# A hybrid decoder step on one core: conv taps from PSUM on two engines, key sums spread anew, query rows by DMA, prompt q/k turned inside units 17 to 24

## The reference

```
h = rmsnorm(x) @ w_in           # 1024 -> conv channels 1536, z 512, b/a 8, q, k, v 512 each, two gates 1024 each
q,k,v of branch A = silu(causal_conv4(conv channels))       # y[t] = sum_i x[t-3+i] * w[i], per channel
branch A = gated DeltaNet(q, k, v, g, beta) -> gated rmsnorm -> w_proj_a
branch B: q, k = partial rope; prompt: causal attention (blocks of 256)
          sample: scores of q with the MEAN of each block of 256 cached keys choose 3 blocks per head,
                  softmax over the chosen blocks and the own row, times cached values; -> w_proj_b
h = x + (sigmoid(ga) * A + sigmoid(gb) * B) @ w_out;  y = h + relu(rmsnorm(h) @ w_up)^2 @ w_down;  final rmsnorm
```

## Time and profile before

| | |
|---|---|
| median of 3 runs | 1262.8 us (1260.28 to 1270.4) |
| span of the profiled execution | 1264.6 us, its first to its last instruction; the change is weighed against this |
| busy share | TensorE 89%, its weight loads 82%, VectorE 53%, ScalarE 36%, GpSimd 20% |
| mean granted clock of TensorE | 0.915 of 2.4 GHz (0.5 is 1.2 GHz) |
| DMA | 151.06 MB, mean 119 GB/s |

### The profile page before, as it was taken

How to read it: one execution, slowest core, us unless ns; L and a number is a source line. 1 busy time by engine, 2 the same in 40 slices (tenths; PEclk the granted TensorE clock), 3 DMA queues, 4 the chain that set the end, 5 groups by cost and what they waited for, 6 DMA issues and landing times.

```text
span 1264.6 us, 21204 instructions
## 1 busy us (share of the span) xinstructions
PE 1125.7 (89%) x8030; PEld 1037.6 (82%) x8030; DVE 674.7 (53%) x906; ACT 460.8 (36%) x686; POOL 257.4 (20%) x112
## 2 busy tenths in 40 slices
PE   4999778787999777997997899999999999999995
PEld 3979778775666666976885879999999999999995
DVE  3526899987643457558554433655533443433433
ACT  3333243333244255455443413324432422522422
POOL 0018455567500006344433000000000000000000
PEclk9989888886579789997997889999999999999998
DMA  7427556566510004464554613432232323232321
GB/s 253 152 65 203 184 184 200 159 201 181 150 43 17 20 25 124 135 183 133 147 153 121 204 34 117 131 120 85 88 97 86 99 85 99 83 99 83 100 66 68
DMA packets 179079, 151.06 MB, mean 119 GB/s; under 512 B 8881, under 2 KB 141555, under 8 KB 178870
## 3 DMA queue, kind: packets, MB, share of 16 engines
q1 hardware_dynamic: 133416, 122.12, 31.9%
q10 hardware_dynamic: 45590, 27.93, 7.7%
HBM read 141.19 MB, written 8.91 MB: 119 GB/s over the span
## 4 chain that ended last, share of the span: by engine, by line
PE 63%; DVE 6%; ACT 4%; issue 2%; POOL 1%; DMA 1%; ACTq 0%; DVEq 0%; POOLq 0%
PE ps L407 44%; PE ps L1729 6%; PE ps L1716 4%; PE ps L1606 2%; PE ps L1616 2%; PE ps L1630 2%; POOL v_low L548 1%; DVE v_low L1212 1%; ACT v_high L783 1%; PE ps L1836 1%; ACT w_high L391 1%; DMA out<-yy 1%; PE ps L1697 1%; PE ps L1823 1%; PE ps L1843 0%
## 5 line engine op out<-in xcount | busy, mean ns | idle before, releaser
L391 ACT ACTIVATE w_high<-w_raw 128x1024 fp32r<-128x1024 f32 x125 | 132.3, 1059 | 461.9 <-PE ps L407 422.8
L407 PE MATMUL ps<-xh,w_high 128*128 128x256 f32 x1232 | 268.9, 301 | 25.9 <-DVE w_low L396 25.9
L407 PE MATMUL ps<-xl,w_high 128*128 128x256 f32 x1232 | 260.3, 294 | 0.0
L407 PE MATMUL ps<-xh,w_low 128*128 128x256 f32 x1232 | 259.4, 293 | 0.0
L396 DVE TENSOR_TENSOR w_low<-w_raw,w_high 128x1024 fp32r<-128x1024 f32 x125 | 162.1, 1297 | 173.9 <-ACT w_high L391 173.6
L407 PEld LDWEIGHTS ps<-xh,w_high 128*128 128x128 f32 x1232 | 204.0, 202 | 37.2 <-DVE w_low L396 21.6
L407 PEld LDWEIGHTS ps<-xl,w_high 128*128 128x128 f32 x1232 | 204.1, 201 | 0.0
L407 PEld LDWEIGHTS ps<-xh,w_low 128*128 128x128 f32 x1232 | 203.0, 199 | 0.0
L531 POOL TENSOR_TENSOR ring<-ring,qb 128x1024 f32<-128x1024 f32 x64 | 162.4, 2555 | 177.3 <-ACT qb L660 90.1
L407 PE MATMUL ps<-mh,w_high 128*128 128x256 f32 (+1 forms) x640 | 129.3, 283 | 2.4 <-issue 2.4
L548 POOL TENSOR_TENSOR v_low<-ring,v_high 128x1024 fp32r<-128x1024 f32 x32 | 79.7, 2490 | 249.3 <-ACT v_high L783 249.3
(11 more groups left out here) (349 smaller groups left out, 1475.5 us busy)
## 6 DMA issues: line engine op xcount, KB each, us to landing
ring<-in_cache_k SPq DMA_DIRECT2D x128, 256.0 KB, 3.2
ring<-in_cache_v SPq DMA_DIRECT2D x128, 256.0 KB, 2.8
w_raw<-in_w_in ACTq DMA_DIRECT2D x82, 256.0 KB, 4.3
w_raw<-in_w_up SPq DMA_DIRECT2D x64, 256.0 KB, 3.1
w_raw<-in_w_down SPq DMA_DIRECT2D x64, 256.0 KB, 3.0
w_raw<-in_w_out SPq DMA_DIRECT2D x16, 256.0 KB, 3.1
ht_dram<-ht ACTq DMA_DIRECT2D x1, 2080.0 KB, 8.1
ht<-ht_dram SPq DMA_DIRECT2D x8, 260.0 KB, 3.6
```

The lines of the kernel that those rows point to most:

```text
L391: act.activation(w_high[:, u % 2], w_raw[:, s], ACT.Copy).then_inc(S_hi, 1)
L407: last = pe.matmul(out[:, a:b], w[:, u % 2, k, :], x[:, i, a:b], start=(first + i == 0 and w is w_high and x is rhs_h), stop=(first + i == ...
```

## The change

- **Conv taps.** `pre` and its zeroing go. ScalarE writes the last tap itself: it copies the sums into `cvr` scaled by that tap's weight (`tap_out`). VectorE adds the other three with the sums read straight from PSUM, each over the columns that have a predecessor. ScalarE waits for the free `cvr` (`tm_turned`), and TensorE's unit u+2 waits for `conv_out` of unit u, because its place in PSUM is read until then. `cvr` moves into the place of `ht`, so its first uses wait for `ht_kept`.
- **Key sums.** None before unit 8; two in units 8 to 12, one or two by turns (18 in 12 units) in 13 to 24, two in 25 to 28: 36. The other 28 are taken in the attention, one a step.
- **Query rows.** The eight matmuls and copies go. SP writes the 8 rotated rows (16 KB) to DRAM and reads them back into all 128 partitions (2 MB), ahead of the fifth key group. GpSimd waits for `qb_landed`.
- **Prompt q/k.** The eight times four transposes and their copies move to units 17 to 24, one each behind `turn_conv`, in banks 6 and 7; ScalarE's wait for the four stores of keys and values moves to unit 17. Gate 0 follows unit 28 directly.

```diff
--- before.py
+++ after.py
 GROUPS = NS * NPAGE // 2
-RED_STEP0 = 6
-RED_T1 = 2 * (N1 - RED_STEP0)
+U_C, U_Z, U_TURN = 13, 25, 17
+
+
+def keys_in_unit(u):
+
+    return 0 if u < 8 else 2 if u < U_C or u >= U_Z else 1 + u % 2
...
+    qb_dram = nc.dram_tensor("qb_dram", [NS, WB], F32, kind="Internal").ap()
...
-        pre = at("pre", [P, 2, 3 + SEQ], F32, r1 + 71872)
-        cvr = at("cvr", [P, 2, SEQ], F32, r1 + 76000)
+        cvr = at("cvr", [P, 2, SEQ], F32, ht_at + 2 * NT * 4)
...
+            def keep_queries():
+
+                sp.wait_ge(*done("rope_q"))
+                sp.dma_start(qb_dram, mts[:, 0:WB]).then_inc(qb_kept, 16)
+                sp.wait_ge(qb_kept, 16)
+                sp.dma_start(qb[:].rearrange("p b c -> p (b c)"),
+                             bc(qb_dram.rearrange("(o b) c -> o (b c)", o=1), [P, NS * WB])).then_inc(qb_landed, 16)
...
                 for r in range(8):
@@ -458,6 +470,8 @@
                         taken, count = low_done(r + 4)
                         sp.wait_ge(taken, b * 4 + (count - 4))
                     elif r >= 4 or not first:
+                        if first and r == 4:
+                            keep_queries()
                         sp.wait_ge(S["k_red"], base + (r - 3))
                     for i in range(2):
...
-            g.wait_ge(S["qb_out"], NS)
+            g.wait_ge(qb_landed, 16)
...
                 elif kind == "c":
                     if j == 0:
-                        act.wait_ge(*done("scr_out"))
-                        act.wait_ge(*done("pre_zero"))
+                        act.wait_ge(ht_kept, 16)
+                        act.wait_ge(*done("own_out"))
                     if j >= 2:
-                        act.wait_ge(S["conv_out"], j - 1)
-                    link(A(pre[:, j % 2, 3:3 + SEQ], unit_ps(u % 2)[:, 0:SEQ], ACT.Copy))
+                        act.wait_ge(S["tm_turned"], j - 1)
+                    A(cvr[:, j % 2], unit_ps(u % 2)[:, 0:SEQ], ACT.Copy,
+                      scale=fw[:, R_CW + 36 + j:R_CW + 37 + j]).then_inc(S["tap_out"], 1)
                     A(tail[:, j], unit_ps(u % 2)[:, SEQ - 3:NT], ACT.Copy).then_inc(unit_out, 1)
                     if j >= 1:
                         silu(j - 1)
@@ -654,10 +669,6 @@
                         conv_turned_out(10)
                     if j == 1:
                         conv_turned_out(11)
-                if u in (5, 6):
-                    for b in range(4 * (u - 5), 4 * (u - 5) + 4):
-                        act.wait_ge(S["qb_sums"], b + 1)
-                        A(qb[:, b], bank(4 + b % 4), ACT.Copy).then_inc(S["qb_out"], 1)
...
+                if U_TURN <= u < U_TURN + 8:
+                    if u == U_TURN:
+                        act.wait_ge(stored_kv, 64)
+                        act.wait_ge(*done("own_out"))
+                        act.wait_ge(qb_kept, 16)
+                        act.wait_ge(*done("ba_out"))
+                    n = u - U_TURN
+                    act.wait_ge(S["qk_turned"], n + 1)
+                    A((qt if n < 4 else kt)[:, n % 4], bank(6 + n % 2), ACT.Copy, scale=ATT_SCALE if n < 4 else 1.0)\
+                        .then_inc(S["qk_out"], 1)
...
-            act.wait_ge(stored_kv, 64)
-            act.wait_ge(*done("own_out"))
-            for n in range(8):
-                act.wait_ge(S["qk_turned"], n + 1)
-                if n == 0:
-                    act.wait_ge(S["conv_out"], 12)
-                    act.wait_ge(*done("ba_out"))
-                A((qt if n < 4 else kt)[:, n % 4], bank(n % 4), ACT.Copy, scale=ATT_SCALE if n < 4 else 1.0)\
-                    .then_inc(S["qk_out"], 1)
-                if n == 3:
-                    gate(0)
+            gate(0)
...
-            v.wait_ge(*done("scr_out"))
-            v.memset(pre[:, :, 0:3], 0.0).then_inc(*did("pre_zero"))
...
             def conv(j):
-                u = 13 + j
+                u = U_C + j
+                v.wait_ge(S["tap_out"], j + 1)
                 v.wait_ge(unit_out, u + 1)
-                if j >= 2:
-                    v.wait_ge(S["tm_turned"], j - 1)
-                c, x = cvr[:, j % 2], pre[:, j % 2]
+                c, x = cvr[:, j % 2], unit_ps(u % 2)
                 w = [fw[:, R_CW + 12 * i + j:R_CW + 12 * i + j + 1] for i in range(CW)]
-                link(TS(c, x[:, 0:SEQ], w[0], None, ALU.mult))
-                link(STT(c, x[:, 1:1 + SEQ], w[1], c, ALU.mult, ALU.add))
-                link(STT(c, x[:, 2:2 + SEQ], w[2], c, ALU.mult, ALU.add))
-                STT(c, x[:, 3:3 + SEQ], w[3], c, ALU.mult, ALU.add).then_inc(S["conv_out"], 1)
+                for back in (1, 2, 3):
+                    ins = STT(c[:, back:SEQ], x[:, 0:SEQ - back], w[3 - back], c[:, back:SEQ], ALU.mult, ALU.add)
+                    if back < 3:
+                        link(ins)
+                    else:
+                        ins.then_inc(S["conv_out"], 1)
...
+                    v.wait_ge(ht_kept, 16)
...
-                if u >= RED_STEP0:
-                    reduce_keys(n_red, 2)
-                    n_red += 2
+                reduce_keys(n_red, keys_in_unit(u))
+                n_red += keys_in_unit(u)
...
-            v.wait_ge(*done("own_out"))
             split_low(v, U_GATE + 2)
...
+            def turn_moba_heads(n):
+                if n == 0:
+                    pe.wait_ge(S["mts_out"], 12)
+                    pe.wait_ge(*done("ba_out"))
+                    pe.wait_ge(S["rope_k"], 2)
+                if n >= 2:
+                    pe.wait_ge(S["qk_out"], n - 1)
+                turn4(6 + n % 2, [mtqk[:, t, n * P:(n + 1) * P] for t in range(4)]).then_inc(S["qk_turned"], 1)
+
             for u, (kind, j, _) in enumerate(UNITS1):
                 pe.wait_ge(S_lo, u + 1)
                 if u >= 2:
                     pe.wait_ge(unit_out, u - 1)
+                if U_C <= u - 2 < U_Z:
+                    pe.wait_ge(S["conv_out"], u - 1 - U_C)
...
-                    pe.wait_ge(*done("rope_q"))
-                if u in (5, 6):
-                    for b in range(4 * (u - 5), 4 * (u - 5) + 4):
-                        if b == 0:
-                            pe.wait_ge(S["mt_out"], 4)
-                            pe.wait_ge(S["mts_out"], 4)
-                        if b == 3:
-                            pe.wait_ge(*done("ba_out"))
-                        if b >= 4:
-                            pe.wait_ge(S["qb_out"], b - 3)
-
-                        mm(bank(4 + b % 4), bc(cf[0:NS, K_ID + b:K_ID + b + 1], [NS, P]), mts[:, 0:WB],
-                           start=True, stop=True).then_inc(S["qb_sums"], 1)
                 if u >= 1 and UNITS1[u - 1][0] in "qkv":
                     turn_moba((u - 1) - (1 if u - 1 > 4 else 0))
                 if kind == "c" and j >= 2:
                     turn_conv(j - 2)
                 if kind == "z" and j < 2:
                     turn_conv(10 + j)
+                if U_TURN <= u < U_TURN + 8:
+                    turn_moba_heads(u - U_TURN)
...
+            pe.wait_ge(S["qk_out"], 8)
+            gate(0)
             pe.wait_ge(unit_out, N1)
-            pe.wait_ge(S["rope_k"], 2)
-            for n in range(8):
-                if n >= 4:
-                    pe.wait_ge(S["qk_out"], n - 3)
-                turn4(n % 4, [mtqk[:, t, n * P:(n + 1) * P] for t in range(4)]).then_inc(S["qk_turned"], 1)
-                if n == 3:
-                    gate(0)
 
             def scores(n):
                 q_t, h = divmod(n, HB)
                 r, N = slice(64 * (h % 2), 64 * (h % 2) + 64), (q_t + 1) * P
-                if n < 3:
-                    pe.wait_ge(S["qk_out"], 8)
-                else:
+                if n == 2:
+                    pe.wait_ge(S["tm_out"], 12)
+                if n >= 3:
                     pe.wait_ge(S["att_exp"], n - 2)
                 mm(score_bank(n, N), qt[r, h // 2, q_t * P:(q_t + 1) * P], kt[r, h // 2, 0:N], start=True, stop=True)\
                     .then_inc(S["att_sums"], 1)
```

12 lines of the change are left out of this document (5 added, 7 removed).

## The result

The changed kernel takes 1219.0 us in the median of four runs (1214.3 to 1221.8), the kernel before 1261.5 on the same chip. The ratio is 0.968, 95% interval 0.964 to 0.972: 3.2% faster. The prediction was 1215 us, in a range of 1201 to 1236, and faster by over 1%. The profiled execution has a span of 1214.4 us, 50.2 less than the 1264.6 of before; the medians differ by 42.6. In every execution that has both on record the time is 1.8 us above the span.

What follows compares the result with a forecast made beforehand. VectorE was taken to bound the conv and z units, TensorE most other stretches. -14.0 - 30.4 - 5.65 + 2 = -48.1 from 1264.6 gave 1216.5, less 1.8 for the median: 1215 us, range 1201 to 1236.

Steps and rivals of the forecast that it cites:

- (a): Units 6 and 7: query rows by DMA instead of matmuls, 12.6 us instead of 26.59, -14.0.
- (e): Attention: key sums go from 18 to 28 and fit VectorE's waits; products may hold dg or w_low, +2 us.
- (c): Conv units, unit 13 to 28: PSUM taps at 0.75 us, TensorE the longer; 100.5 against 130.89 us, -30.4.
- (b): Units 8 to 12: time from unit 7 to 13 left as it was; up to 4 us could go by luck.
- rival C: Conv units: taps from PSUM wait for GpSimd all the same, +60 us, 1275; chance 0.05.
- the slips: Units 13 to 28: 3 us added to 97.5 for new waits, among them held w_low and a late conv(2).
- (d): Hand-over from unit 28's end to the attention's first exp: 10.05 us instead of 15.7, -5.65.
- rival B: Attention steps 9 to 17: clock stays at 2.4 GHz, some 8 us shorter, 1205 with some luck; chance 0.07.
- Rivals A: Conv units stay fed too slowly and settle at 7.5 us, adding 12 us: 1227; chance 0.14.
- D: Conv stage never bound by VectorE, TensorE's gaps from key loads; only (a) and (d) count: 1243; chance 0.05.

Runs made afterwards that it cites:

- e9: Kernel before with only the query rows by DMA (eight matmuls and copies gone): 1248.3 us, ratio 0.990.
- e6: Changed kernel with the small gate instructions early, key rotation spread over units 10 to 12, some key sums moved, store of k in unit 13: 1209.8 us, ratio 0.962.
- e4: Kernel before with GpSimd's products over 16 of their 1024 columns: 1213.5 us, ratio 0.963.
- e10: Changed kernel with GpSimd's products over 16 of their 1024 columns: 1204.8 us, ratio 0.955.
- e2: Changed kernel with ScalarE copying to SBUF again and four VectorE taps reading there: 1234.3 us, ratio 0.978.
- the square: Four kernels: before and changed, each with full and with small GpSimd products; unit 13 to 28 took 130.9, 103.5, 92.8 (before, small) and 96.9 us (changed, small).
- e5: Changed kernel with VectorE's three small gate instructions moved from unit 13 to behind the copy of ba after unit 4: 1213.8 us, ratio 0.965.
- e11: Changed kernel with the prompt's q and k turned behind unit 28 as before, not in units 17 to 24: 1217.0 us, ratio 0.963.
- e3: Changed kernel with two key sums in every unit from 8 on, 22 left for the attention: 1218.5 us, ratio 0.964.
- e7: Changed kernel with the attention's diagonal (dg) made by ScalarE instead of VectorE: 1222.0 us, ratio 0.973.
- e8: Changed kernel with the edits of e6 and e7 together: 1213.5 us, ratio 0.965.

## Why the prediction was right

The largest part came by the mechanism named: taps that read PSUM are not held, and TensorE sets the pace of the conv units. For (a) and (e) the number was better than the reason. 48.1 us were forecast; 50.2 came in the spans and 42.6 in the medians, whose interval allows 36 to 46. So 48.1 is a little too much, and the closeness of the spans is in part luck: before was profiled in one of its longer executions, after in one of its shorter, and the errors of the parts cancel, 3.0 us of gain too much in (c) against 1.5 too little in (b), 2.5 in (e) and 1.1 in the rest. The 1.8 us that I took off for the median are by the later runs what an execution takes beyond its span, not what a median lies below it; for the forecast this changes nothing, since it is the median of before less 48.1 either way.

(a) 14.0 forecast, 14.0 measured (26.59 to 12.63), and e9 gives it by itself. But the matmuls are not short, as I called them: they took 8.4 of the 14.0 us, and the low clock cost the two products 4.8. The row that I read shows five of their sixteen instructions. The forecast didn't need the split, since it took the whole difference to two undisturbed units. The clock did fall without a hole: from 78 to 83 us of before TensorE is busy all the time and the granted clock is 0.53, right behind the first group of 8-row matmuls. The broadcast took 6.9 us, nearer the 8.1 of the store of its size than the 19.6 of four times wf; the 16 KB before it, taken at 3.2, were over in at most 2.3 (issue at 70.82, next issue at 73.16), close to the 2 us of the Trainium skill, DMA: Bandwidth & Descriptors, section Latency and other measured facts.

(b) Left as it was, with up to 4 us of luck: 1.5 less. That the hole behind unit 12 would stay was right (6.9 us); e6 shows that it needs the rotation, e4 and e10 that it needs the products beside it.

(c) 100.5 forecast, 103.5 measured. The taps at 0.75 are right to the hundredth, and rival C is dead: e2 and the square show that the place of one operand decides. The Trainium skill, VectorE: DVE Perf Modes, section Rules for kernel authors, has to copy to SBUF first as one of two ways if many operations follow; here that form costs 17.9 us more (e2). The Trainium skill, SBUF — State Buffer, section Who interferes with whom, gives the reason, and the traces agree: two SBUF inputs, up to 2.85 us; one in PSUM, 0.751 at most. The step that was mis-sized is the slips. I allowed 3 us over the ideal 97.5: 0.34 a unit for w_low and 1 us late for conv(2) in unit 14. Measured are 6.9 over four undisturbed units up to T(17), and 0.9 under the estimate behind it. w_low was held (1.75 us in the mean of the stage's 15) and cost nothing behind unit 17, where TensorE has no wait: its 6.65 hides it. What cost was what I had not looked at: three 20-column instructions in unit 13, held for 6.9 us in all, and the 5 us hole and low clock behind them; e5 took 4.9 us of it away. I had read a held pair of 8 x 64 instructions in the rotation, but didn't ask which other short ones lie beside four products in a row.

(d) 5.65 forecast, 5.62 measured; e11 gives 5.85 and the price in the units, 3.6 by the unit and 4.3 by the marks, for the 3.9 of the sum.

(e) +2 forecast, -0.5 measured, and the reason was half right. That held dg instructions would be felt is true: their mean went from 386 to 739 ns, and TensorE waits 15.3 us for them (7.3 before). The chain of waits shows it. Of 294 to 348 us before, then of 246 to 300 us after:

```profile
by line: PE ps L1606 24.2%; PE ps L1616 19.1%; PE ps L407 17.8%; PE ps L1630 17.6%; DVE lg L977 10.8%; issue 4.4%; DVE ps L1093 2.5%; DVE nbias L1096 1.8%; DVE dg L1083 1.7%; DVE rrs L1080 0.6%
```

```profile
by line: DVE lg L986 25.2%; issue 19.3%; PE ps L411 10.6%; DVE dg L1093 9.9%; PE ps L1608 8.1%; PE ps L1618 7.3%; PE ps L1632 6.5%; DVE ps L1102 5.8%; DVE nbias L1105 2.4%; ACT w_high L395 2.0%; DVE rrs L1090 1.8%; DVE onb_l L1084 1.3%; ACT
```

VectorE, not TensorE, ends last in the first half now. I had argued that the key sums fit into VectorE's waits; in that half they don't. The attention is as long all the same, and the clock there is 0.70, not 0.53: some of what rival B named came, in the same steps. The two were not separated by a run, and the change isn't shown to be the cause of either. e9, with 18 sums and no part of the change but the query rows, has the same picture in the first 54 us of its attention, while e3, with 22 sums and the whole change beside, has that of before (0.53, VectorE 40.77):

```profile
275.30:329.30 54.00, 45.61 (x173) 30.71 (x173) 48.08 (x89) 15.91 (x54) 35.95 (x16) 0.66 0.63 184
```

What decides between the two pictures stays open. With 18, 22 and 28 sums the attention took 112.5 to 117.3, 118.1 and 112.3 to 117.0 us (e7 and e8 aside), so the count of sums doesn't show over its scatter.

Rivals A (units at 7.5) and D (not bound by VectorE) are refuted by the 6.65 and by e2 and e4. The median of 1219.0 is 4 us above the 1215 forecast; the profiled execution took 1216.2, and the four lie between 1214.3 and 1221.8. Only the one was traced, so where the others lost time isn't known.

## What to carry to other kernels

Read minimum, median and maximum of an instruction beside its mean: a mean twice the minimum with maxima one neighbour's instruction long is waiting, and where the operands lie can remove it without less work. Then look for the shortest instructions on the same queue that still have only SBUF operands, and place them where the neighbour idles; a mean over many units doesn't show them, the differences of unit marks do. Judge an edit by the marks of its stage before the span: here the unchanged rest moved by more than several of the edits were worth. And compare a sum from two profiled executions with the medians too: here the spans gave 50.2 us and the medians 42.6.

## What was not expected of the hardware

What a GpSimd product held up doesn't depend on the size of the held instruction: 128 x 20 took 2.29 to 2.33 us, and 0.18 where GpSimd was idle. For TENSOR_SCALAR one SBUF input is enough (2.32 for 128 x 20, up to 2.62 for 128 x 512 in e2). Yet the 64 key sums, reductions that also read SBUF only, stayed within 1.198 and 1.222 us beside the same products, and a tap with one input in PSUM and the other and its output in SBUF was never held in 36. It goes the other way too: the product that starts at 133.65, 0.13 us behind a w_low, took 3.35 us, the three after it 2.4 each. A broadcast of 16 KB from DRAM to 128 partitions, 2 MB written, landed in 6.9 us, while 512 KB of wf took 4.9.
